# The last four units of the two-tile output products done tile by tile, in a two-block transformer kernel

## The chip, the cores and the metric

The kernel runs on one core of one Trainium2 chip. The metric is the time of one execution on the device, in microseconds, as the median of several runs.

## The reference

Everything is fp32 and the width is 1024. First a block of two layers on 256 positions: normed rows through an attention mixer and an output product, then a gated feed-forward product. Then a second block of two layers on the 256 positions and on 256 context positions; each of its sub-layers is computed like this, with `j` = 0 a feed-forward, 1 a mixer (attention and a gated spatial product), 2 a feed-forward:

```python
def adaln_in(s, g_pre, shift, scale):
    return rmsnorm(s, g_pre) * (1 + scale) + shift
def adaln_out(s, y, g_post, gate, weight):
    return s + weight * gate * rmsnorm(y, g_post)
def ffn_sublayer(s, mod, j, g_pre, g_post, wg, wu, wd):
    y = adaln_in(s, g_pre, mod[..., 3 * j, :, :], mod[..., 3 * j + 1, :, :])
    return adaln_out(s, swiglu(y, wg, wu, wd), g_post, mod[..., 3 * j + 2, :, :], FFN_RES)
```

So the output of a sub-layer needs the mean square of a whole row of `y` before it can be added to `x`, and the next sub-layer needs the mean square of the whole new row of `x` before its first product.

## The kernel before, in words

The program is one list of ten sub-layers (`SUBS`, numbered from 0). Positions lie in tiles of 128 rows: tiles 0 and 1 are the 256 positions, 2 and 3 the context. From sub-layer 4 on the tiles form two streams, the leading one (`LEAD`, tiles 2 and 3) and the trailing one (`TRAIL`, tiles 0 and 1). Sub-layers 4 to 7 carry two tiles per stream up to their end (`tt` is 4); they are followed by sub-layers 5 to 8, which begin with two tiles per stream. These are four handovers.

Every product is fp32 in three passes: each operand is split into a rounded high part and a low part, and the matmuls are high times high, high times low and low times high. Weights come in units of 128 x 1024 through a ring of four slots: a DMA fills `raw`, ScalarE makes `whi` (`split_hi`, L1003), VectorE makes `wlo` (`split_lo`, L1478). A slot is free again when the trailing stream has used the unit (`unit_done`).

A sub-layer has a wide part and a tall part. The wide part multiplies the transposed input (`xhi`, `xlo`) with chunks of four units, per chunk first the leading and then the trailing stream. The tall part is the output product. It adds up 8 or 22 units in PSUM, two banks per tile, banks 0 to 3 for the leading stream and 4 to 7 for the trailing one. Its units are taken in groups, in each group first a leading pass and then a trailing pass (`tall_pass`); a unit is 12 matmuls of 128 x 512 (two tiles, two halves, three products). Its activations are split per unit and stream into `ahi` and `alo` (`share_hi` L1015, `share_lo` L1701), in four places that the two streams use in turn, so that a share of the trailing pass waits for the leading pass's unit of the same number.

The order on each engine is written out by hand; semaphores join them. At a handover, for each stream:

- ScalarE squares the finished tile half by half with a running sum (`square_y`, L1104), VectorE multiplies it by the gain into `rows` (`add_y2`, L1624), GpSimd takes the inverse root (`inverse_root`, L2154), VectorE adds to `x` (L1633). ScalarE and VectorE never read the same PSUM half at once, and wait for one another between the halves.
- ScalarE squares the new row (`square_x`, L1089), GpSimd takes the root again, VectorE writes the normed row into `rows` (`normed_row`, L1519).
- TensorE transposes the normed rows into PSUM (`transposes_in`, L585, 8 per tile). Those of the leading stream stand ahead of the last unit of the trailing tall pass, those of the trailing stream ahead of unit 3 of the next sub-layer's first wide pass.
- ScalarE and VectorE turn the transposed pieces into the wide operand (`operand_hi`, `operand_lo`): eight pieces of 128 x 256, each scaled and shifted into `fbuf` (pieces 2, 3, 6, 7 on ScalarE, L1031; 0, 1, 4, 5 on VectorE, L1533), rounded (L1041) and the rest taken (L1543). The first wide unit waits for pieces 0 to 3 to be scaled and 0 and 1 to be split, unit `u` for pieces up to `2u + 1`. The next sub-layer's first four weight units are split in between.

## Time and profile before

| | |
|---|---|
| median of 3 runs | 2564.03 us (2563.63 to 2567.45) |
| the profiled execution | 2570.65 us, span 2568.8 us |
| TensorE busy | 2464.2 us (96%), 11536 matmuls |
| VectorE, ScalarE, GpSimd busy | 1145.1 (45%), 1064.4 (41%), 167.4 (7%) |
| mean granted TensorE clock | 0.980 |

The span is from the first to the last instruction that the profiler saw; the execution's own time has 1.85 us more around it. A matmul's end in the profile is modelled, and successive matmuls overlap, so work on TensorE is read from the starts. A granted clock of 1.00 is 2.4 GHz and 0.50 is 1.2 GHz.

### The profile page before, as it was taken

What the parts mean: (1) busy time and instruction counts of PE and PEld (TensorE: products, weight loads), DVE (VectorE), ACT (ScalarE), POOL (GpSimd) and SP (SyncE); (2) the same over time, 40 slices, a digit from 0 to 9 for tenths busy, and PEclk for the clock granted to TensorE, in tenths of its full rate; (3) what the DMA queues carried; (4) which work ended last, traced back from release to release, by engine and by line L of the source; (5) the groups of instructions that cost most, each with busy time, mean ns of one, the idle gap of its engine ahead of it and who ended that gap; (6) DMA issues with size and microseconds to landing.
All of it is one profiled execution on the core that took longest, in us unless ns stands there. A gap on an engine that the chain in (4) does not pass through costs nothing. (4 is left out here: it accounts for less than half of the span.)

```text
span 2568.8 us, 29909 instructions
## 1 busy us (share of the span) xinstructions
PE 2464.2 (96%) x11536; PEld 1939.5 (76%) x11536; DVE 1145.1 (45%) x1960; ACT 1064.4 (41%) x1945; POOL 167.4 (7%) x205
## 2 busy tenths in 40 slices
PE   8999999999999999999989999999999999987998
PEld 6766777766877778877677777887778887766777
DVE  5554455634552223354745222345222335455455
ACT  6443456434542223344545222334222334454544
POOL 1100003000010000022101000001000001310000
PEclk9999999999999999999989999999999999997999
DMA  5557654387534533232103444332432222312554
GB/s 207 184 205 286 229 180 141 123 302 281 189 125 163 173 122 99 91 114 66 58 25 131 157 171 163 100 107 74 174 109 95 99 87 94 115 58 74 172 181 147
DMA packets 118733, 364.40 MB, mean 142 GB/s; under 512 B 11072, under 2 KB 11712, under 8 KB 118592
## 3 DMA queue, kind: packets, MB, share of 16 engines
q1 hardware_dynamic: 116336, 355.62, 40.4%
q0 software_dynamic: 2256, 6.86, 1.1%
q8 instruction: 93, 1.52, 0.2%
q14 instruction: 48, 0.39, 0.1%
HBM read 361.35 MB, written 1.09 MB: 141 GB/s over the span
## 5 line engine op out<-in xcount | busy, mean ns | idle before, releaser
L1478 DVE TENSOR_TENSOR wlo<-raw,whi 128x1024 fp32r<-128x1024 f32 x524 | 644.0, 1234 | 620.1 <-ACT whi L1003 615.5
L562 PE MATMUL ps<-whi,xhi 128*128 128x512 f32 x2096 | 854.6, 408 | 12.5 <-DVE xlo L1570 5.0
L562 PE MATMUL ps<-whi,xlo 128*128 128x512 f32 x2096 | 823.6, 393 | 0.0
L562 PE MATMUL ps<-wlo,xhi 128*128 128x512 f32 x2096 | 821.8, 392 | 0.0
L1003 ACT CAST whi<-raw 128x1024 fp32r<-128x1024 f32 x524 | 549.2, 1051 | 511.0 <-PE ps L562 502.5
L562 PEld LDWEIGHTS ps<-whi,xhi 128*128 128x128 f32 x2096 | 397.9, 190 | 151.8 <-issue 66.1
L562 PEld LDWEIGHTS ps<-whi,xlo 128*128 128x128 f32 x2096 | 396.4, 189 | 87.9
L562 PEld LDWEIGHTS ps<-wlo,xhi 128*128 128x128 f32 x2096 | 398.2, 190 | 73.4
L562 PE MATMUL ps<-whi,ahi 128*128 128x512 f32 x952 | 375.8, 395 | 12.0 <-DVE alo L1701 7.7
L562 PE MATMUL ps<-whi,alo 128*128 128x512 f32 x952 | 373.1, 392 | 0.0
L562 PE MATMUL ps<-wlo,ahi 128*128 128x512 f32 x952 | 372.9, 392 | 0.0
L562 PEld LDWEIGHTS ps<-whi,ahi 128*128 128x128 f32 x952 | 180.1, 189 | 51.4 <-issue 5.9
L562 PEld LDWEIGHTS ps<-whi,alo 128*128 128x128 f32 x952 | 180.2, 189 | 38.1
L562 PEld LDWEIGHTS ps<-wlo,ahi 128*128 128x128 f32 x952 | 180.5, 190 | 36.5
L1692 DVE TENSOR_TENSOR hrow<-sgate,ps 128x256 f32<-128x256 f32 x154 | 58.6, 416 | 299.4 <-ACT sgate L1156 298.0
L1015 ACT CAST ahi<-hid 128x128 fp32r<-128x128 f32 (+1 forms) x264 | 86.7, 351 | 218.2 <-PE ps L562 218.0
L2154 POOL TENSOR_TENSOR rstd<-ms,mhalf 128x1 f32<-128x1 f32 (+1 forms) x55 | 41.3, 751 | 2000.4 <-DVE ms L1628 1430.1
L1701 DVE TENSOR_TENSOR alo<-hid,ahi 128x128 fp32r<-128x128 f32 (+1 forms) x264 | 88.6, 355 | 179.2 <-ACT ahi L1015 179.2
L1164 ACT COPY hid<-ps 128x256 f32<-128x256 f32 x198 | 67.0, 372 | 190.1 <-PE ps L621 190.1
L1156 ACT ACTIVATE sgate<-ps 128x256 f32<-128x256 f32 x154 | 51.5, 379 | 175.8 <-PE ps L562 175.8
L562 PE MATMUL ps<-mraw,cstat 128*32 128x512 f32 x576 | 76.7, 605 | 0.0
L621 PEld LDWEIGHTS ps<-ident,hrow 128*128 128x128 f32 x396 | 48.2, 140 | 33.3 <-DVE hrow L1689 14.2
(153 smaller groups left out, 1409.4 us busy)
## 6 DMA issues: line engine op xcount, KB each, us to landing
raw<-in_w SPq DMA_DIRECT2D x524, 512.0 KB, 3.8
mraw<-in_w_mod SPq DMA_DIRECT2D x72, 1024.0 KB, 6.6
grow<-gains POOLq DMA_DIRECT2D x11, 512.0 KB, 5.3
x<-in_x SPq DMA_DIRECT2D x2, 512.0 KB, 5.2
x<-in_ctx SPq DMA_DIRECT2D x1, 1024.0 KB, 7.8
out<-x SPq DMA_DIRECT2D x2, 512.0 KB, 2.6
rmask<-in_rmask SPq DMA_DIRECT2D x1, 768.0 KB, 4.9
ws<-in_ws POOLq DMA_DIRECT2D x2, 256.0 KB, 5.9
```

The source lines that it names most:

```text
L562: return nc.tensor.matmul(o, lhsT, rhs, start=start, stop=stop, skip_group_check=True)
L621: last = nc.tensor.transpose(bank(wide_bank(s, c, st, i), P * h, P * h + P), hrow[:, 2 * st + i, P * h:P * h + P], ident[:, :])
L1003: nc.scalar.copy(whi[:, slot, :], raw[:, slot, :]).then_inc(hi_done, 1)
L1015: nc.scalar.copy(ahi[:, w * aslot:w * aslot + w], src[:, row, P * tiles[0]:P * tiles[0] + w]).then_inc(a_hi_done, 1)
L1156: nc.scalar.activation(sgate[:, 2 * st + i, :], bank(wide_bank(s, c, st, i), 0, 256), ACT.Silu, **late).then_inc(silu_done, 1)
L1164: nc.scalar.copy(hid[:, 2 * c:2 * c + 2, P * t:P * t + P], src).then_inc(chunk_taken, 1)
L1478: nc.vector.tensor_tensor(wlo[:, slot, :], raw[:, slot, :], whi[:, slot, :].bitcast(F32), ALU.subtract).then_inc(w_split, 1)
L1692: nc.vector.tensor_tensor(hrow[:, 2 * st + i, :], sgate[:, 2 * st + i, :], up, ALU.mult).then_inc(gate_done, 1)
L1701: nc.vector.tensor_tensor(alo[:, w * aslot:w * aslot + w], src[:, row, P * tiles[0]:P * tiles[0] + w], ahi[:, w * aslot:w * aslot + w].bit ...
L2154: nc.gpsimd.tensor_tensor(rstd[:, m0:m], ms[:, m0:m], mhalf[:, m0:m], ALU.pow).then_inc(rstd_ready, 1)
```

## The change

In sub-layers 4 to 7 the last group of the tall part (four units, `by_tile`) is done in both passes first for the stream's first tile in all four units and then for its second tile. The first tile of each stream is therefore complete in the middle of the pass, and a unit counts as done when its second tile is. The leading transposes stand ahead of the last two units of the second tile, with the same twelve matmuls behind them as before. `square_y` and `add_y2` are cut into functions of one tile. On ScalarE and VectorE, output, addition and new row of each tile are put elsewhere: the leading first tile's among the trailing shares, the trailing first tile's ahead of and inside the next operand's pieces, the trailing second tile's wholly inside them. GpSimd takes the roots in the new order. Sub-layers 8 and 9 and the first block keep their order.

```diff
--- before.py
+++ after.py
+def by_tile(s, g):
+    return s["tt"] == 4 and g == len(s["groups"]) - 1
...
-                for k in group:
+                turns = [(k, (0, 1)[:len(tiles)]) for k in group]
+                if by_tile(s, g):
+                    turns = [(k, (i,)) for i in range(2) for k in group]
+                for k, which in turns:
...
+                    if by_tile(s, g):
+                        if nxt is not None and st == TRAIL and k == s["k"] - 2 and which == (1,):
+                            transposes_in(nxt, LEAD)
+                    elif nxt is not None and st == TRAIL and k == s["k"] - 4 + before_the_end(nxt):
                         transposes_in(nxt, LEAD)
...
-                    for i, t in enumerate(tiles):
+                    for i in which:
...
                         if final and i < len(tiles) - 1:
                             last.then_inc(y_ready, 1)
-                    last.then_inc(unit_done, 1)
+                    if len(tiles) - 1 in which:
+                        last.then_inc(unit_done, 1)
...
-            def operand_hi(s, st):
+            def operand_hi(s, st, trail=None):
...
                     scaled(2)
                     high(0)
                     high(1)
+                    if trail:
+                        square_x(trail["tall"][TRAIL][0], X_AT[trail["i"], trail["tall"][TRAIL][0]])
                     scaled(3)
                     high(2)
                     if st == LEAD:
                         split_hi(s["u_wide"] + 2)
-                    for k in (3, 4, 5):
+                    high(3)
+                    if trail:
+                        square_tile(trail, TRAIL, 1)
+                    for k in (4, 5):
                         high(k)
                     if st == LEAD:
                         split_hi(s["u_wide"] + 3)
                     scaled(7)
                     high(6)
                     high(7)
+                    if trail:
+                        square_x(trail["tall"][TRAIL][1], X_AT[trail["i"], trail["tall"][TRAIL][1]])
...
+            def square_tile(s, st, i):
+                tiles = s["tall"][st]
+                t = tiles[i]
+                if i < len(tiles) - 1:
+                    act.wait_ge(y_ready, n["y"] + 1)
+                    n["y"] += 1
+                else:
+                    act.wait_ge(unit_done, DONE[s["u_tall"] + s["k"] - 1, st])
+                for h in range(2):
...
+                    nc.scalar.activation(squares[:, t, CH * h:CH * h + CH], bank(tall_bank(st, i) + h), ACT.Square,
+                                         scale=D ** -0.5, accum_out=sqy[:, t, h:h + 1]).then_inc(sqy_halves, 1)
+                n["z"] += 1
             def square_y(s, st):
-                tiles = s["tall"][st]
...
+                for i in range(len(s["tall"][st])):
+                    square_tile(s, st, i)
...
+                if s is not None and s["tt"] == 4:
+                    if st == LEAD:
+                        square_tile(s, LEAD, 1)
+                        square_x(tiles[1], X_AT[s["i"], tiles[1]])
+                        square_tile(s, TRAIL, 0)
+                        split_hi(nxt["u_wide"])
+                        split_hi(nxt["u_wide"] + 1)
+                    operand_hi(nxt, st, s if st == LEAD else None)
+                    return
                 if s is not None and s["blk"] == 2:
                     square_y(s, st)
...
+                        if by_tile(s, g) and st == TRAIL:
+                            square_tile(s, LEAD, 0)
+                            for k in group[:3]:
+                                share_hi(s, k, TRAIL)
+                            square_x(s["tall"][LEAD][0], X_AT[s["i"], s["tall"][LEAD][0]])
+                            share_hi(s, group[3], TRAIL)
                             continue
...
-            def operand_lo(s, st):
+            def operand_lo(s, st, trail=None):
...
                     scaled(1)
                     low(0)
                     low(1)
+                    if trail:
+                        mean_square(trail["tall"][TRAIL][0])
+                        split_lo(s["u_wide"] + 1)
                     dve.wait_ge(xs_ready, s["xs0"][st] + 2)
                     scaled(4)
                     scaled(5)
@@ -1554,12 +1597,20 @@
                     if st == LEAD:
                         split_lo(s["u_wide"] + 2)
                     low(3)
+                    if trail:
+                        normed_tile(trail, TRAIL, 0)
+                        out_tile(trail, TRAIL, 1)
                     low(4)
                     low(5)
+                    if trail:
+                        add_tile(trail, TRAIL, 1)
                     if st == LEAD:
                         split_lo(s["u_wide"] + 3)
                     low(6)
                     low(7)
+                    if trail:
+                        mean_square(trail["tall"][TRAIL][1])
+                        normed_tile(trail, TRAIL, 1)
...
+            def out_tile(s, st, i):
+                dve.wait_ge(grow_ready, 16 * n["g"])
+                if i < len(tiles) - 1:
+                    dve.wait_ge(y_ready, n["y"] + 1)
+                    n["y"] += 1
+                else:
+                    dve.wait_ge(unit_done, DONE[s["u_tall"] + s["k"] - 1, st])
+                for h in (1, 0):
...
+                    nc.vector.tensor_tensor(rows[:, t, CH * h:CH * h + CH], bank(tall_bank(st, i) + h),
+                                            grow[:, ctx_of(tiles), CH * h:CH * h + CH], ALU.mult).then_inc(z_halves, 1)
+                n["z"] += 1
+                dve.wait_ge(sqy_halves, 2 * n["z"])
+                nc.vector.scalar_tensor_tensor(ms[:, t:t + 1], sqy[:, t, 0:1], EPS, sqy[:, t, 1:2], ALU.add,
+                                               ALU.add).then_inc(ms_ready, 1)
+            def add_tile(s, st, i):
+                t = s["tall"][st][i]
+                dve.wait_ge(z_halves, 2 * n["z"])
+                rstd_wait()
+                nc.vector.scalar_tensor_tensor(x[:, t, :], rows[:, t, :], rstd[:, t:t + 1], x[:, t, :],
+                                               ALU.mult, ALU.add).then_inc(x_ready, 1)
+
+            def normed_tile(s, st, i):
+                t = s["tall"][st][i]
+                dve.wait_ge(x_ready, X_AT[s["i"], t])
+                normed_row(t)
...
+                for i in range(len(s["tall"][st])):
+                    out_tile(s, st, i)
+                for i in range(len(s["tall"][st])):
+                    add_tile(s, st, i)
...
+                if s is not None and s["tt"] == 4:
+                    if st == LEAD:
+                        out_tile(s, LEAD, 1)
+                        normed_tile(s, LEAD, 0)
+                        add_tile(s, LEAD, 1)
+                        mean_square(tiles[1])
+                        normed_tile(s, LEAD, 1)
+                        out_tile(s, TRAIL, 0)
+                        split_lo(first)
+                        add_tile(s, TRAIL, 0)
+                    operand_lo(nxt, st, s if st == LEAD else None)
+                    return
...
+                        if by_tile(s, g) and st == TRAIL:
+                            out_tile(s, LEAD, 0)
+                            share_lo(s, group[0], TRAIL)
+                            share_lo(s, group[1], TRAIL)
+                            add_tile(s, LEAD, 0)
+                            share_lo(s, group[2], TRAIL)
+                            share_lo(s, group[3], TRAIL)
+                            mean_square(s["tall"][LEAD][0])
+                            continue
...
                 for st in (LEAD, TRAIL):
+                    if s["tt"] == 4:
+
+                        for t in s["tall"][st]:
+                            inverse_roots([t, t])
+                        continue
```

On VectorE, what stands between the last shares of the trailing pass and the next operand, at the first handover, before (`alo` are shares, `wlo` weight splits, `ms` a mean square, `rows<-ps,grow` the output by the gain, `rows<-x,rstd` the normed row):

```order
L1624 TENSOR_TENSOR rows<-ps,grow 128x512 x2
L1628 SCALAR_TENSOR_TENSOR ms<-sqy 128x1
L1624 TENSOR_TENSOR rows<-ps,grow 128x512 x2
L1628 SCALAR_TENSOR_TENSOR ms<-sqy 128x1
L1633 SCALAR_TENSOR_TENSOR x<-rows,rstd,x 128x1024 x2
L1507 TENSOR_SCALAR ms<-sq 128x1
L1519 TENSOR_SCALAR rows<-x,rstd 128x1024
L1507 TENSOR_SCALAR ms<-sq 128x1
L1519 TENSOR_SCALAR rows<-x,rstd 128x1024
L1478 TENSOR_TENSOR wlo<-raw,whi 128x1024 x2
```

and the beginning of the same stretch in the change, from the first instruction behind the leading shares:

```order
L1675 TENSOR_TENSOR rows<-ps,grow 128x512 x2
L1679 SCALAR_TENSOR_TENSOR ms<-sqy 128x1
L1779 TENSOR_TENSOR alo<-hid,ahi 128x256 x2
L1687 SCALAR_TENSOR_TENSOR x<-rows,rstd,x 128x1024
L1779 TENSOR_TENSOR alo<-hid,ahi 128x256 x2
L1547 TENSOR_SCALAR ms<-sq 128x1
L1675 TENSOR_TENSOR rows<-ps,grow 128x512 x2
L1679 SCALAR_TENSOR_TENSOR ms<-sqy 128x1
L1559 TENSOR_SCALAR rows<-x,rstd 128x1024
L1687 SCALAR_TENSOR_TENSOR x<-rows,rstd,x 128x1024
L1547 TENSOR_SCALAR ms<-sq 128x1
L1559 TENSOR_SCALAR rows<-x,rstd 128x1024
```

The leading first tile's output now stands ahead of the trailing shares and its addition between them; the second tile's output follows all of them, each tile's normed row and addition alternate, and no weight split stands here any more.

On ScalarE, the operand of the next sub-layer's leading stream, before (`fbuf` are scaled pieces, `xhi` the high parts, `whi` weight splits, `squares` the squares of a finished tile of `y`, `rows,sq<-x` the square of a new row):

```order
L1031 ACTIVATE fbuf<-ps,modT,acol 128x256
L1041 CAST xhi<-fbuf 128x256 x2
L1031 ACTIVATE fbuf<-ps,modT,acol 128x256
L1041 CAST xhi<-fbuf 128x256
L1003 CAST whi<-raw 128x1024
L1041 CAST xhi<-fbuf 128x256 x3
L1003 CAST whi<-raw 128x1024
L1031 ACTIVATE fbuf<-ps,modT,acol 128x256 x2
L1041 CAST xhi<-fbuf 128x256 x2
L1104 ACTIVATE squares,sqy<-ps 128x512 x4
```

and in the change, from the trailing first tile's squares on:

```order
L1123 ACTIVATE squares,sqy<-ps 128x512 x2
L1015 CAST whi<-raw 128x1024 x2
L1043 ACTIVATE fbuf<-ps,modT,acol 128x256
L1053 CAST xhi<-fbuf 128x256 x2
L1108 ACTIVATE rows,sq<-x 128x1024
L1043 ACTIVATE fbuf<-ps,modT,acol 128x256
L1053 CAST xhi<-fbuf 128x256
L1015 CAST whi<-raw 128x1024
L1053 CAST xhi<-fbuf 128x256
L1123 ACTIVATE squares,sqy<-ps 128x512 x2
L1053 CAST xhi<-fbuf 128x256 x2
L1015 CAST whi<-raw 128x1024
```

Two weight splits stand directly ahead of the operand and behind the trailing first tile's squares; the square of its new row is between the first high parts and the next scaled piece, and the second tile's squares are in the middle of the high parts.

On VectorE, the same operand before (`xlo` are the low parts):

```order
L1533 TENSOR_SCALAR fbuf<-ps,acol,modT 128x256 x2
L1543 TENSOR_TENSOR xlo<-fbuf,xhi 128x256 x2
L1533 TENSOR_SCALAR fbuf<-ps,acol,modT 128x256 x2
L1543 TENSOR_TENSOR xlo<-fbuf,xhi 128x256
L1478 TENSOR_TENSOR wlo<-raw,whi 128x1024
L1543 TENSOR_TENSOR xlo<-fbuf,xhi 128x256 x3
L1478 TENSOR_TENSOR wlo<-raw,whi 128x1024
L1543 TENSOR_TENSOR xlo<-fbuf,xhi 128x256 x2
```

and in the change:

```order
L1573 TENSOR_SCALAR fbuf<-ps,acol,modT 128x256 x2
L1583 TENSOR_TENSOR xlo<-fbuf,xhi 128x256 x2
L1547 TENSOR_SCALAR ms<-sq 128x1
L1518 TENSOR_TENSOR wlo<-raw,whi 128x1024
L1573 TENSOR_SCALAR fbuf<-ps,acol,modT 128x256 x2
L1583 TENSOR_TENSOR xlo<-fbuf,xhi 128x256
L1518 TENSOR_TENSOR wlo<-raw,whi 128x1024
L1583 TENSOR_TENSOR xlo<-fbuf,xhi 128x256
L1559 TENSOR_SCALAR rows<-x,rstd 128x1024
L1675 TENSOR_TENSOR rows<-ps,grow 128x512 x2
L1679 SCALAR_TENSOR_TENSOR ms<-sqy 128x1
L1583 TENSOR_TENSOR xlo<-fbuf,xhi 128x256 x2
```

A weight split, a normed row and the second tile's output came in between the low parts.

## Rows read from the trace of the kernel before

**Rows 1.** The page: busy time of each engine, its share, instructions.
```profile
PE 2464.2 (96%) x11536; PEld 1939.5 (76%) x11536; DVE 1145.1 (45%) x1960; ACT 1064.4 (41%) x1945; POOL 167.4 (7%) x205
```

**Rows 2.** Timeline of TensorE, first handover: start, duration, engine, line, instruction, idle before.
```profile
1111.78 0.39 PE L562 MATMUL ps<-whi,alo 128*128 128x512 f32 x1
...
1118.20 0.47 PE L562 MATMUL ps<-whi,xhi 128*128 128x512 f32 x1 [0.33 <-ACT fbuf L1031]
...
1126.15 0.39 PE L562 MATMUL ps<-wlo,xhi 128*128 128x512 f32 x1
1126.38 0.39 PE L562 MATMUL ps<-whi,xlo 128*128 128x512 f32 x1
...
1130.94 1.10 PE L585 MATMUL ps<-ident,rows 128*128 128x128 f32 x8 [4.17 <-DVE rows L1519]
...
1134.11 0.78 PE L562 MATMUL ps<-whi,xhi 128*128 128x512 f32 x1
1134.68 0.63 PE L562 MATMUL ps<-wlo,xhi 128*128 128x512 f32 x1
```

**Rows 3.** Timeline of TensorE at the second, third and fourth handover.
```profile
1366.56 0.39 PE L562 MATMUL ps<-whi,alo 128*128 128x512 f32 x1
...
1389.06 0.78 PE L562 MATMUL ps<-whi,xhi 128*128 128x512 f32 x1
...
1770.49 0.39 PE L562 MATMUL ps<-whi,alo 128*128 128x512 f32 x1
...
1792.82 0.78 PE L562 MATMUL ps<-whi,xhi 128*128 128x512 f32 x1
...
2163.11 0.39 PE L562 MATMUL ps<-whi,alo 128*128 128x512 f32 x1
...
2185.97 0.78 PE L562 MATMUL ps<-whi,xhi 128*128 128x512 f32 x1
```

**Rows 4.** Table by stretch: length, busy time (count) per engine, TensorE clock, DMA.
```profile
1131.90:1135.30 3.40, 2.95 (x13) 2.62 (x12) 2.21 (x5) 1.57 (x5) 1.91 (x2) 0.50 0.29 2
...
1384.50:1391.30 6.80, 5.57 (x21) 5.13 (x22) 4.27 (x10) 3.41 (x9) 3.10 (x4) 0.50 0.17 2
```

**Rows 5.** Timelines of ScalarE, VectorE and GpSimd, leading stream of the first handover.
```profile
1104.36 0.60 ACT L1104 ACTIVATE squares<-ps 128x512 f32<-128x512 f32 x1
...
1104.85 0.19 ACT L1104 ACTIVATION_READ_ACCUMULATOR squares<-ps 128x1 f32 x1
...
1106.34 1.28 DVE L1624 TENSOR_TENSOR rows<-ps,grow 128x512 f32<-128x512 f32 x2
...
1106.51 0.56 POOL L2154 TENSOR_TENSOR rstd<-ms,mhalf 128x1 f32<-128x1 f32 x1 [366.80 <-DVE ms L1628]
...
1107.65 1.04 ACT L1003 CAST whi<-raw 128x1024 fp32r<-128x1024 f32 x1
...
1107.87 1.28 DVE L1633 SCALAR_TENSOR_TENSOR x<-rows,rstd,x 128x1024 f32<-128x1024 f32 x1
...
1108.02 1.55 POOL L2154 TENSOR_TENSOR rstd<-ms,mhalf 128x1 f32<-128x1 f32 x1 [0.95 <-DVE ms L1628]
...
1109.19 1.06 ACT L1089 ACTIVATE rows<-x 128x1024 f32<-128x1024 f32 x1 [0.51 <-DVE x L1633]
...
1111.68 0.75 DVE L1519 TENSOR_SCALAR rows<-x,rstd 128x1024 f32<-128x1024 f32 x1 [0.73 <-POOL rstd L2154]
...
1113.89 2.35 DVE L1478 TENSOR_TENSOR wlo<-raw,whi 128x1024 fp32r<-128x1024 f32 x2
...
1114.81 0.57 ACT L1031 ACTIVATE fbuf<-ps,modT,acol 128x256 f32<-128x256 f32 x1 [1.80 <-PE ps L585]
...
1116.16 0.99 DVE L1533 TENSOR_SCALAR fbuf<-ps,acol,modT 128x256 f32<-128x256 f32 x2
...
1116.73 0.86 ACT L1041 CAST xhi<-fbuf 128x256 fp32r<-128x256 f32 x2 [1.36 <-DVE fbuf L1533]
...
1117.17 0.88 DVE L1543 TENSOR_TENSOR xlo<-fbuf,xhi 128x256 fp32r<-128x256 f32 x2
```

42 lines of the change are left out of this document (7 added, 35 removed).

## The prediction

> **What bounds the kernel now.** I read the page first: TensorE is busy for 96% of the span and no other engine for half of it [rows 1]. So the time is TensorE's queue, and a change that adds or removes no matmul can only move the places where that queue stands still. Four of them are touched: the handovers out of the four sub-layers whose products have two tiles per stream (4 to 5, 5 to 6, 6 to 7, 7 to 8 in the program's count). I read TensorE's timeline at the first. One 512-column matmul follows another every 0.227 us (1126.15 to 1126.38 in [rows 2]), so a half unit of 6 takes 1.36 us, a unit of 12 takes 2.72, a group of four 10.88; 8 transposes take 0.87 (1.10 shown, less the tail that overlaps). The reader is to see in [rows 2]: 6.42 us from the last matmul before the leading stream's transposes (1111.78) to the first wide matmul (1118.20), in which lie 4.69 of work (0.23, 16 transposes, 12 matmuls), so 1.73 lost, 0.33 of it idle at its very end; and an idle time of 4.17 before the trailing stream's transposes, ended by VectorE's normed row. I add up the whole: from 1111.78 to the first matmul of wide unit 3 (1134.11) there are 0.23 + 1.74 (16 transposes) + 2.72 + 8.16 + 1.74 = 14.60 us of work, and 22.33 passed: 7.73 lost. The same difference at the others is 22.50, 22.33 and 22.86 [rows 3], so 7.9, 7.7 and 8.3 are lost; together 31.6. After that come matmuls at the half clock: in [rows 4] the granted clock is 0.50, that is 1.2 GHz, for 3.4 us at the first handover and for 6.8 at the second; the third is like the first, the fourth like the second. From unit 3 on this costs about 0.6, 1.2, 0.6 and 1.9 us (0.35 for the first matmul, 1134.11 to 1134.68 in [rows 2], and 0.2 for each further one until the low stretch ends, whose duration is 0.63 there against 0.39). All that the change can reach is 31.6 + 4.3 = 36 us, 1.4% of the time.
>
> **Why VectorE and ScalarE are late.** Each tile's new row is a chain through both, one tile after another. Prices from the first handover [rows 5]: square of half a tile 0.68 with its accumulator read (next may start after 0.58), gain product of half a tile 0.68 (0.60), the two squares' sum 0.16, root on GpSimd 0.56, addition 1.28, square of x 1.15 (1.06), normed row 0.75, weight split 1.04 on ScalarE (0.95) and 1.22 on VectorE (1.14), scaled piece 0.57 on ScalarE and 0.54 on VectorE, high part 0.41 (0.31), low part 0.42 (0.34), and a share, of the same size, the same on both. A handoff between engines costs 0.03 to 0.1. One root took 1.55 instead of 0.56: VectorE's addition had begun 0.15 before it and ended at 1109.15, and the root ended 0.41 later. I charge that delay wherever a root meets a long VectorE instruction on SBUF.
>
> **The change, on one handover.** I set T = 0 at the start of the leading pass of the last group, 1092.96 in the trace (1111.78 + 0.23 less seven units of 2.72), and lay each engine's new list out in order with the prices above. As a test, the same bookkeeping on the old lists gives TensorE waits of 0.56, 0.68, 0.59, 0.13, 4.55 and 0.68, 7.2 us, and the trailing transposes at T = 38.18; the trace has them at 1130.94, T = 37.98. It is 0.2 us late after 38 and does not know the clock.
>
> *The leading pass.* TensorE's matmuls are the same ones in another order, so its work costs nothing more. It asks for share and weights of the last unit at T = 4.08 instead of 8.16. Their split ends at 2.81 (slot free at 0.20, share 0.31, split 1.04, then 1.22): 1.1 us of cover, no wait. The same 12 matmuls stand behind the leading transposes.
>
> *Leading stream.* Tile 0 is finished at 5.44 and not 8.16. Its squares and gain products run 5.64 to 7.05, its addition stands behind two shares whose slots come free only with units 0 and 1 of tile 1, and runs 9.15 to 10.43; square 10.47 to 11.62. The last trailing share is queued behind that square: 11.53 to 12.40 over both engines, wanted at 14.96, so covered. Tile 1: products 12.39 to 13.67, addition 15.18 to 16.46 (its root meets the normed row of tile 0), square to 17.65, normed row 18.57 to 19.33. TensorE wants tile 0's row at 19.04 (there since 14.66) and tile 1's at 19.91. Both waits go: 1.1 us gained.
>
> *Trailing tile 0.* Finished at 16.32, but VectorE takes it up after that normed row: products 19.24 to 20.53. ScalarE stands in its second square until 20.65, then makes the first two weight splits to 22.54. VectorE: split 21.63 to 22.85, addition 22.76 to 24.05, two scaled pieces to 24.96, and ScalarE's two high parts to 25.40. Now ScalarE's square of x (25.31 to 26.46) stands ahead of the scaled piece 3, which ends at 26.92. The first wide matmul needs that piece: it starts at 27.06, where TensorE was ready at 23.51. **A wait of 3.56 us in place of 0.59**: this is what the change pays.
>
> *Inside the first three wide units.* VectorE: split of unit 1 to 27.78, pieces 4 and 5 to 28.70, low part 2, split of unit 2 to 30.17, low part 3 to 30.51, so unit 1 starts at 30.65 instead of 29.78 (0.86 lost). Normed row of trailing tile 0, 30.42 to 31.17; products of tile 1, 31.09 to 32.37, with ScalarE held in its second square to 32.50; high parts 4 and 5, low parts to 33.59, so unit 2 starts 0.36 late at 33.73. Addition 33.50 to 34.79, split of unit 3 to 35.92, square of x 35.50 to 36.65, root, normed row 37.57 to 38.33.
>
> *Trailing transposes.* Unit 2 ends at 36.45, tile 0's row is long there, 8 transposes to 37.32, tile 1's start at 38.38: 1.06 lost. Unit 3 starts at 39.25, on the trace's clock 1132.21 and not 1134.11. So 5.8 us are lost to waits where 7.7 were.
>
> **The sum.** Four times 5.84 is 23.4 against 31.6: 8.2 us. The low clock goes from unit 3, for by then TensorE has worked nearly without a pause since T = 27: up to 4.3 us. It may fall behind the 3.56 wait instead. There a low stretch of 3.4 us costs 1.7 us of matmul time, but the waits of 0.86, 0.36 and 1.06 behind it are ends of the VectorE and ScalarE chain, which does not wait for TensorE there, and swallow 2.3; I charge 0.3 per handover for the cases of 6.8 us. The bookkeeping's bias gives 0.2 each back. 8.2 + 4.3 - 1.2 + 0.8 = 12.1, rounded to **12 us**. The profiled execution (2570.65, span 2568.8) would become 2558.6; it stands 6.6 above the median of 2564.03, so I predict **2552 us**. Weight loads into the ring start 0.7 to 6 us later (they follow the VectorE splits), and are first wanted 13 us after the handover; I cost them at nothing. No engine gets an instruction more.
>
> **The root and the shared port.** The row of 1.55 us shows the delay [rows 5]. The Trainium skill, "SBUF — State Buffer", section "SBUF: two separate sides", says that GpSimd and a VectorE instruction with two SBUF inputs take one port pair by an exclusive lock, so that the later one blocks fully; by that rule the change is worse than the old order, since its roots meet a VectorE that works without gaps. The trace agrees for the one root that met an addition.
>
> **Rivals.**
> *The roots wait for VectorE to stand still* (a mechanism of the new order: additions and splits back to back). Trailing tile 0's root is issued at T = 26.73 inside 4 us of unbroken VectorE work; if it only gets through when VectorE stops for it, its normed row is 0.6 late, and the root of tile 1 makes its addition 0.6 late. For: the 1.55 row. Against: between two instructions there was room in every other row. 1.2 us on four handovers takes 5 of the 12: **2557**. Chance 0.20, two fifths of it inside 0.2%.
> *The low clock is not swallowed*: it falls at the 3.56 wait for 6.8 us everywhere, 3.4 lost less 2.3, and the transposes run in it too (1.7 more): 2.8 more on each handover, which takes 11: **2563**, no change. Chance 0.08.
> *The clock stays low through the whole handover*, the way to slower: four waits within 12 us instead of one, each feeding the next low stretch. From the wait at T = 23.5 on, low for 13.6 us costs 6.8 less 2.3 swallowed, 4.5 on top of 5.8: 10.3 against 9.0, 4 times 1.3 slower: **2569**. It decides from some 11 us of low clock per handover. Against it: no stretch in [rows 4] is over 6.8, and the clock stayed full behind the 1.73 us lost around the leading transposes [rows 2]. The Trainium skill, "TensorE: Matmul & The Clock Gate", section "HAM oscillation — how this bites in real kernels", has this as a rule: pauses between short batches bring every batch back to the cold clock; no run here shows it for waits as short as 1 us. Chance 0.08.
> *The first wait is shorter* because handoffs overlap more than I charge, or a root is not delayed by a normed row (0.5 less): each us on the chain is 4 us of time, so 17 or more are saved: **2546**. Chance 0.09.
> The forecast keeps 0.55.
>
> **Numbers.** A measurement of this kernel tells about 0.2% (5.1 us) from no change. Faster by more: 0.55 + 0.12 + 0.09 = 0.76; within it 0.16; slower 0.08. For 8 in 10 the range must hold the forecast, the rival of the roots and part of the shorter wait: from 2546 (18 saved) to 2560.5 (3.5 saved).
>
> **What would show it.** In the changed profile, at each handover: no idle time, or under 0.2 us, before the leading transposes; about 3.3 to 3.6 us ended by ScalarE's scaled piece or VectorE before the first wide matmul; no 4 us wait before the trailing transposes but about 1 us, before the second tile's; low clock, if any, directly behind the first wide matmul and not at unit 3. From the end of the leading transposes' last unit to wide unit 3, 15.7 us. I am wrong if the long wait is gone without a new one ahead of the first wide unit (more gain), or if the chain to the trailing tile 1's row takes longer than T = 39.5.

## The result, and the profile after

The change made the kernel faster by about as much as forecast. It takes 2549.33 us (median of four executions, 2546.97 to 2551.56) where the kernel before takes 2565.62 (2563.63 to 2567.45): a ratio of 0.9937, 95% interval 0.9919 to 0.9954, 16.3 us less; 2552 was forecast. The four executions of the changed kernel are two pairs, at 2547.0 and 2551.5, and the median lies between them. Profiled executions: 2570.65 us before, 2547.14 after (span 2545.3, mean granted clock 0.988 where it was 0.980).

TensorE is still the only full engine. The page of the changed kernel, against [rows 1]:

```profile
PE 2447.3 (96%) x11536; PEld 1926.0 (76%) x11536; DVE 1145.1 (45%) x1960; ACT 1062.0 (42%) x1945; POOL 165.1 (6%) x205
```

TensorE's timeline at the first handover of the changed kernel, against [rows 2]; the columns are the same:

```profile
1106.93 0.39 PE L567 MATMUL ps<-whi,alo 128*128 128x512 f32 x1
...
1107.17 1.91 PE L590 MATMUL ps<-ident,rows 128*128 128x128 f32 x16
...
1115.09 0.47 PE L567 MATMUL ps<-whi,xhi 128*128 128x512 f32 x1 [3.27 <-ACT fbuf L1043]
...
1118.67 0.47 PE L567 MATMUL ps<-whi,xhi 128*128 128x512 f32 x1 [0.57 <-DVE xlo L1583]
...
1121.74 0.47 PE L567 MATMUL ps<-whi,xhi 128*128 128x512 f32 x1
...
1124.56 1.03 PE L590 MATMUL ps<-ident,rows 128*128 128x128 f32 x8
1126.35 1.09 PE L590 MATMUL ps<-ident,rows 128*128 128x128 f32 x8 [0.76 <-DVE rows L1559]
1127.20 0.48 PE L567 MATMUL ps<-whi,xhi 128*128 128x512 f32 x1
```

The 16 leading transposes follow the last matmul at once. The wait of 4.17 us ahead of the trailing transposes is gone; in its place stand idle times of 3.27 us ahead of the first wide matmul, 0.57 ahead of unit 1, next to nothing ahead of unit 2, and 0.76 ahead of the second tile's transposes. From 1106.93 to unit 3 at 1127.20 pass 20.27 us, against 22.33 before.

The same two matmuls at the second, third and fourth handover, against [rows 3]:

```profile
1359.63 0.40 PE L567 MATMUL ps<-whi,alo 128*128 128x512 f32 x1
...
1379.90 0.48 PE L567 MATMUL ps<-whi,xhi 128*128 128x512 f32 x1
...
1760.31 0.40 PE L567 MATMUL ps<-whi,alo 128*128 128x512 f32 x1
...
1780.57 0.47 PE L567 MATMUL ps<-whi,xhi 128*128 128x512 f32 x1
...
2150.33 0.39 PE L567 MATMUL ps<-whi,alo 128*128 128x512 f32 x1
...
2170.59 0.48 PE L567 MATMUL ps<-whi,xhi 128*128 128x512 f32 x1
```

They are 20.27, 20.26 and 20.26 us apart. Less the 14.60 us of work, 5.7 us are lost at each handover, where 7.73, 7.9, 7.7 and 8.3 were.

The granted clock, in the table by stretch of the changed kernel, against [rows 4]: the whole neighbourhood of the first and second handover, and the only low stretches at the third and fourth.

```profile
1085.00:1145.00 60.00, 55.33 (x258) 45.16 (x257) 38.42 (x65) 32.83 (x68) 11.74 (x17) 1.00 0.34 111
1345.00:1400.00 55.00, 50.29 (x240) 41.03 (x239) 36.05 (x64) 31.11 (x68) 9.06 (x12) 1.00 0.42 142
1769.00:1772.40 3.40, 3.40 (x9) 2.65 (x8) 3.40 (x7) 1.45 (x4) 0.58 (x1) 0.50 0.46 154
2158.10:2161.50 3.40, 3.02 (x7) 2.50 (x8) 3.40 (x6) 2.37 (x6) 1.45 (x1) 0.50 0.37 110
```

At the first two the clock is full (2.4 GHz) throughout; at the others it is at 1.2 GHz for 3.4 us behind the first wait, and still the four handovers take the same time to 0.01 us. The later waits show why: those ahead of units 1 and 2 (0.73 and 0.23 us from start to start at the first handover) are gone at the third and fourth, and the one ahead of the second tile's transposes shrank from 0.76 to 0.52.

```profile
2169.74 1.09 PE L590 MATMUL ps<-ident,rows 128*128 128x128 f32 x8 [0.52 <-DVE rows L1559]
```

VectorE, ScalarE and GpSimd of the changed kernel, the chain that ends the first wait, against [rows 5]:

```profile
1102.13 1.00 POOL L2242 TENSOR_TENSOR rstd<-ms,mhalf 128x1 f32<-128x1 f32 x1 [0.96 <-DVE ms L1679]
...
1107.30 1.28 DVE L1675 TENSOR_TENSOR rows<-ps,grow 128x512 f32<-128x512 f32 x2
...
1108.02 0.60 ACT L1123 ACTIVATE squares<-ps 128x512 f32<-128x512 f32 x1 [1.73 <-DVE rows L1675]
1108.61 1.99 ACT L1015 CAST whi<-raw 128x1024 fp32r<-128x1024 f32 x2
1109.67 1.23 DVE L1518 TENSOR_TENSOR wlo<-raw,whi 128x1024 fp32r<-128x1024 f32 x1 [0.78 <-ACT whi L1015]
1110.82 1.28 DVE L1687 SCALAR_TENSOR_TENSOR x<-rows,rstd,x 128x1024 f32<-128x1024 f32 x1
1112.01 0.99 DVE L1573 TENSOR_SCALAR fbuf<-ps,acol,modT 128x256 f32<-128x256 f32 x2
...
1113.35 1.05 ACT L1108 ACTIVATE rows<-x 128x1024 f32<-128x1024 f32 x1
1114.40 0.55 ACT L1043 ACTIVATE fbuf<-ps,modT,acol 128x256 f32<-128x256 f32 x1
...
1114.76 1.46 POOL L2242 TENSOR_TENSOR rstd<-ms,mhalf 128x1 f32<-128x1 f32 x1 [5.24 <-DVE ms L1547]
```

The forecast's T = 0 is 1088.12 here (1106.93 + 0.23 less seven units). It had trailing tile 0's products at 19.24, the addition at 22.76, the square of x at 25.31 and the first wide matmul at 27.06; the rows give 19.18, 22.70, 25.23 and 26.97.

### The profile page after: what moved, and what is told of

Same layout as the page of the kernel before. It is cut to its first block and busy times, and to the rows that moved or that the text cites. A ratio compares the mean times of both kernels' runs of the same rounds, so it can differ in the third digit from the quotient of the medians.

```text
span 2545.3 us, 29957 instructions
## 1 busy us (share of the span) xinstructions
PE 2447.3 (96%) x11536; PEld 1926.0 (76%) x11536; DVE 1145.1 (45%) x1960; ACT 1062.0 (42%) x1945; POOL 165.1 (6%) x205
```

## Where the rest of the time went

For all kernels below I use one measure: at each handover, the time from the start of the 84th instruction ahead of the leading transposes to that of the 25th behind the trailing ones, less 156 matmuls of 0.2267 us and 32 transposes of 0.109. This difference counts waits and low clock together. Where I give a wait "from start to start", it is the spacing of two starts less that of two successive instructions; the idle time in a row is shorter, since it begins at the modelled end of the instruction before. Summed over the four handovers it is 36.17 us before (8.40, 9.04, 8.43, 10.30) and 23.13 after (5.78, 5.78, 5.79, 5.77): **13.0 us**, where 12 were forecast. The profiled executions differ by 23.5 and the medians by 16.3, so 3 to 10 us are elsewhere. By the spacings above, 9.0 of the 13.0 lie ahead of unit 3; the other 4 lie behind it, where the kernel before had its low clock. TensorE runs the same 11536 instructions in both, so I took the stretches between the same numbers of them. The two traces of each kernel, profiled time first (the second ones are experiments below):

```
                                     before  before    after   after
profiled time                       2570.65 2567.11  2547.14 2551.46
four handovers, lost                  36.17   36.12    23.13   23.85
instructions     0 to  2216          493.01  489.86   489.10  488.47
              2216 to  4909          584.66  584.70   583.54  583.38
              5153 to  6132          200.05  200.05   200.59  199.00
             10336 to 10630           64.17   62.58    57.09   63.82
```

Instructions 10336 to 10630 are the mixer of sub-layer 8, which the change doesn't touch. There the changed kernel's first trace has a low stretch of 3.4 us, and the kernel before one of 20.5:

```profile
2308.30:2311.70 3.40, 3.00 (x7) 2.45 (x8) 1.67 (x8) 0.00 (x0) 0.00 (x0) 0.50 0.00 0
```

```profile
2316.30:2336.80 20.50, 18.05 (x74) 16.98 (x75) 8.00 (x34) 3.72 (x13) 1.64 (x1) 0.50 0.00 0
```

These instructions alone take 7.1 us less in the changed kernel's profiled execution. The experiments on the repeated traces ask whether the change earned it.

## Experiments

**TensorE's order alone.** The kernel before with tile-by-tile turns and the leading transposes at their new place; VectorE, ScalarE and GpSimd keep their old order.

```
+                turns = [(k, (0, 1)[:len(tiles)]) for k in group]
+                if by_tile(s, g):
+                    turns = [(k, (i,)) for i in range(2) for k in group]
```

> TensorE's tile-by-tile order of the last group alone, with the old orders on ScalarE, VectorE and GpSimd. Theory (the handover ends with a chain through ScalarE and VectorE, and TensorE's order by itself brings nothing): the trailing shares now wait for the second tile's units and everything behind them stays put, so the leading chain starts late: waits of about 2.7, 0.7, 0.6, 0.1, 4.6, 0.7 us, 9.3 us per handover where the kernel before has 7.2 by the same bookkeeping, and the half clock at unit 3 stays. Four handovers: about 8 us slower than before, 2573 to 2575. Rival (the gain comes from finishing the first tile in the middle of the pass): faster than before by 4 us or more.

Measured: 2570.18 us, ratio 1.0019 (1.0010 to 1.0029): 5.5 above the 2564.69 of the kernel before in that session, slower as expected but short of the 8 that I expected. Handovers 45.45 us, 9.3 more; in its profiled execution the last mixer gave 7 back (57.12 us for 64.17). TensorE's timeline of this kernel:

```profile
1110.67 3.51 PE L590 MATMUL ps<-ident,rows 128*128 128x128 f32 x16 [2.50 <-DVE rows L1531]
...
1129.11 3.67 PE L590 MATMUL ps<-ident,rows 128*128 128x128 f32 x16 [3.83 <-DVE rows L1531]
```

The first wait came as forecast (2.66 in start-to-start times). The trailing one is shorter, about 4.0 where 4.6 was expected, and those of 0.6 and 0.7 are down to 0 and 0.1. Low clock ahead of a wait that VectorE ends would do that, but no run separates it from the bookkeeping's error (4.55 for 4.33 in the kernel before). And 10.2 us of low clock per handover, three times the 3.4 of the first handover before, slow the transposes themselves (3.51 us for 16 against 1.91). TensorE's order brings nothing without the others.

**Leading stream alone.** The changed kernel with the trailing stream's early work put back behind the leading stream's.

```
-                        square_tile(s, TRAIL, 0)
...
-                        out_tile(s, TRAIL, 0)
                         split_lo(first)
-                        add_tile(s, TRAIL, 0)
+                        split_lo(first + 1)
```

> The leading stream's part of the change alone (TensorE's order of both passes, output, addition and rows of both leading tiles in the new places); the trailing tiles' work stands in one piece behind the operand, as in the kernel before. Theory: the waits ahead of the leading transposes and of the first wide unit go (0 to 0.2 us left), the wait of 4.4 us before the trailing transposes stays whole, 0.7 before the second tile's. By waits alone that is 5.4 us per handover, less than the 5.8 of the full change; but the one long wait is again followed by the half clock, which here nothing swallows: 1.4 to 3.5 us on each handover. So about 7 to 8 us lost per handover, 4 to 8 us faster than before and 4 to 9 slower than the full change: 2554 to 2561. Rival (the trailing part buys time by itself, the clock has little to do with it): the waits at full clock are longer than 5.8 us per handover. Rival (the trailing part is worthless): as fast as the full change within 1 us per handover.

Measured: 2554.28 us, ratio 0.9956 (0.9942 to 0.9971). Handovers 28.17 us (7.40, 7.52, 6.09, 7.16), 8.0 less than before. No wait ahead of the leading transposes, none over 0.1 us ahead of the wide units, and the old one at its old place:

```profile
1106.62 1.91 PE L590 MATMUL ps<-ident,rows 128*128 128x128 f32 x16
...
1123.92 3.67 PE L590 MATMUL ps<-ident,rows 128*128 128x128 f32 x16 [4.26 <-DVE rows L1562]
```

So 8 of the 13 us come from the leading stream's part and 5 from the trailing one, but not by shorter waits. By waits alone this kernel is the better one: from start to start it has 4.42 and 0.10 us at the first handover, where the full change has 3.43, 0.73, 0.23 and 0.92. What it loses beyond them is low clock, 6.8 us of it at three handovers and 3.4 at the third, which also loses the least (6.09). The trailing part moves the long wait forward, to where the low clock behind it is taken up by the waits that follow.

**Output in the gap.** The trailing tile's first product goes ahead of the leading tile 1's mean square and its second ahead of the normed row, where VectorE waits for ScalarE and the root.

```
-                        mean_square(tiles[1])
-                        normed_tile(s, LEAD, 1)
-                        out_tile(s, TRAIL, 0)
+                        out_tile(s, TRAIL, 0, "first")
+                        mean_square(tiles[1])
+                        out_tile(s, TRAIL, 0, "second")
+                        normed_tile(s, LEAD, 1)
+                        out_tile(s, TRAIL, 0, "sum")
```

> The full change, and the gain products of trailing tile 0 moved ahead of the normed row of leading tile 1 (the first before its mean square, the second before the row), where VectorE stands waiting for ScalarE and GpSimd. Theory (one chain through both engines from trailing tile 0 to the last normed row sets the end, each us on it is a us of each handover): all of it 1.2 us earlier, the wait ahead of the first wide unit 2.3 us where the full change has 3.4, the later ones the same 0.7, 0.3, 0.9: 1.2 us per handover, 5 us less than the full change. Rival (the waits within the wide units are set by the weight splits and not by the chain): less than 0.4 us per handover.

Measured: 2547.13 us (2544.58 to 2548.42), ratio 0.9927 (0.9912 to 0.9942). Handovers 15.90 us, 1.8 less each and not 1.2; the wait is 1.61 from start to start, where 2.3 was expected:

```profile
1109.82 0.47 PE L567 MATMUL ps<-whi,xhi 128*128 128x512 f32 x1 [1.45 <-ACT fbuf L1043]
```

My bookkeeping charges a root that meets a long VectorE instruction on SBUF. The root of trailing tile 0's output began 0.02 us ahead of the weight split here, and neither is longer than usual by more than 0.03, so that delay did not come:

```profile
1104.36 0.54 POOL L2257 TENSOR_TENSOR rstd<-ms,mhalf 128x1 f32<-128x1 f32 x1 [1.30 <-DVE ms L1667]
```

```profile
1104.38 1.25 DVE L1518 TENSOR_TENSOR wlo<-raw,whi 128x1024 fp32r<-128x1024 f32 x1
```

But of 7.2 us saved at the handovers the profiled time kept 1.2. Instructions 10336 to 10630 took 63.95 us here, with 20.5 us of low clock. Either this order disturbs the last mixer, or that stretch comes and goes by itself; this is taken up below.

**Square of x behind the scaled piece.** ScalarE does the piece that the first wide matmul waits for first.

```
-                    if trail:
-                        square_x(trail["tall"][TRAIL][0], X_AT[trail["i"], trail["tall"][TRAIL][0]])
                     scaled(3)
+                    if trail:
+                        square_x(trail["tall"][TRAIL][0], X_AT[trail["i"], trail["tall"][TRAIL][0]])
```

> The full change, with ScalarE's square of trailing tile 0's new row behind the scaled piece 3 and not ahead of it. It is the instruction that stands ahead of the piece for which the first wide unit waits. Theory (the end is set by the chain, what happens to TensorE in between is swallowed): the first wait falls from 3.4 to about 2.4 us, the second grows from 0.7 to about 2.3, and as the chain gets 0.5 us longer the handover loses 0.5 more in sum: 2 us slower than the full change on four handovers. Rival (the wait ahead of the first wide unit is a cost by itself): 1 us per handover faster, 4 us in sum.

Measured: 2557.46 us, ratio 0.9972 (0.9960 to 0.9983). At the first and third handover the two waits are as forecast, 2.4 and 2.2 from start to start:

```profile
1112.67 0.47 PE L567 MATMUL ps<-whi,xhi 128*128 128x512 f32 x1 [2.23 <-ACT fbuf L1043]
...
1117.74 0.47 PE L567 MATMUL ps<-whi,xhi 128*128 128x512 f32 x1 [2.07 <-DVE xlo L1583]
```

At the second and fourth, 3.4 us of low clock lie between the two, and the second wait is 0.7: again the clock is paid out of it. Handovers 25.58, 2.4 us more than in the changed kernel, close to the forecast of 2. The wait that goes returns one unit later, behind the same square. The other 6 us of the median's difference lie outside the handovers; in the profiled execution 7.0 of them are in the last mixer (64.05 us for 57.09).

**Extra work in the chain, and ahead of it.** Two more products of half a tile, in the trailing stream's tile-0 output or in the leading stream's.

```
+                        for _ in range(2 if s["tt"] == 4 and (st, i) == (TRAIL, 0) else 0):
+                            link(nc.vector.tensor_tensor(rows[:, t, 0:CH], bank(tall_bank(st, i)),
+                                                         grow[:, ctx_of(tiles), 0:CH], ALU.mult))
```

> The changed kernel with two extra gain products of half a tile (about 0.68 us each, nothing reads them twice) on VectorE inside the trailing stream's tile-0 output at each handover. My theory (VectorE's chain through this output to the first weight split ends TensorE's first wait, with 0.66 us of slack in front of the second half, where it waits for ScalarE's squares): the wait ahead of wide unit 0 grows from 3.4 to about 4.1 us, the others stay, 6.5 us per handover, 3 us in all. Rival A (VectorE has no slack there): 4.8 us, 7.2 per handover, 5.5 us in all. Rival B (the first wait is set by ScalarE's squares and parts): it stays at 3.4 us.

> The changed kernel with two extra gain products of half a tile (about 0.68 us each) on VectorE inside the LEADING stream's tile-0 output, which lies some 12 us ahead of TensorE's first wait. Theory (VectorE stands idle behind this output, waiting for ScalarE's squares and TensorE's units, and takes the extra work in there): the waits stay at 3.4, 0.7, 0.2 and 0.9 us, 5.8 per handover. Rival (VectorE's work is one unbroken chain from there to the first weight split): the first wait is 1.36 us longer, 7.2 per handover.

Measured, one execution each: 2558.79 and 2555.71 us. In the trailing output the first wait is 4.37 where it was 3.43, 0.94 longer, between the 0.70 of my theory and the 1.36 of the rival; the handovers are 6.71, 6.93, 7.41 and 6.71 us. The trace shows that the theory came near for a wrong reason:

```profile
1109.43 1.46 POOL L2245 TENSOR_TENSOR rstd<-ms,mhalf 128x1 f32<-128x1 f32 x1 [3.65 <-DVE ms L1682]
```

```profile
1111.00 1.28 DVE L1690 SCALAR_TENSOR_TENSOR x<-rows,rstd,x 128x1024 f32<-128x1024 f32 x1 [0.52 <-POOL rstd L2245]
```

VectorE had more slack than I thought, and its weight split began only 0.34 us later. But the root now met that split, took 1.46 us where it had taken 0.54, and VectorE stood idle for 0.52 ahead of the addition. So by the trace a delayed root did reach TensorE here, for some 0.6 us at the first handover.

In the leading output, where I expected nothing, the first wait is 3.73, 0.30 longer, and the handovers are 6.10, 6.77, 6.09 and 6.77. The trace of that kernel shows the path: the leading addition comes 0.30 us later behind the output, ScalarE's square of x with it, and behind that square stand the last share and the squares of tile 1. VectorE's gaps take 1.06 of the 1.36 us, not all. The chain that ends the first wait thus begins some 20 us ahead of that end, on both engines.

**The same kernel once more.** No edit.

> The changed kernel once more, with no edit, for a second trace. Two of its four executions took 4.4 us more than the two others. Theory (half-clock stretches outside the handovers come and go between executions of one kernel): the handovers again lose 5.8 us each, 23.1 in all, whatever the time; if the profiled execution takes about 2551.5 us, the difference lies in the last mixer (stretch of 57.09 us in the first trace) and ahead of the first handover. Rival (the handovers themselves vary, by a wait of another length): a slower execution has handovers of 6.5 us and more.

> The kernel before once more, with no edit. The profiled execution of before took 2570.65 us where the median is 2564 to 2566. Theory: its handovers lose again 8.4 to 10.3 us each, about 36 in all, and any difference in time lies in the half-clock stretches outside them: 584.66 us ahead of the first handover and 64.17 us in the last mixer can come out at 583.6 and 57 to 59. Rival: the handovers take less, 30 us in all.

Measured: the changed kernel 2548.26 us (2546.66 to 2551.46), ratio 0.9932 (0.9916 to 0.9949). Its profiled execution took 2551.46 us, 4.3 more than the first trace, and the handovers 23.85 (5.79, 6.48, 5.79, 5.79). The three others had 3.4 us of low clock each and lost nothing by it; the second had 6.8, and the waits behind it couldn't swallow it all: 0.7 passed through. To that extent the rival of the expectation is right too. The difference is in the last mixer, 63.82 us for 57.09, less 2.4 us gained ahead of the second handover. Its low stretch:

```profile
2296.50:2317.00 20.50, 17.27 (x73) 16.37 (x74) 8.66 (x36) 4.50 (x14) 1.71 (x2) 0.50 0.01 6
```

The kernel before took 2567.11, with handovers of 36.12 against 36.17. Its last mixer stayed long, 62.58 us, and instructions 2216 to 4909 took what they had; of the 3.5 us between its two traces, 3.15 are in the first 2216 instructions. I had expected them elsewhere.

**Early output at three handovers, or at the fourth only.**

```
-                        out_tile(s, TRAIL, 0, "first")
+                        if s["i"] != 7:
+                            out_tile(s, TRAIL, 0, "first")
...
+                        else:
+                            mean_square(tiles[1])
+                            normed_tile(s, LEAD, 1)
+                            out_tile(s, TRAIL, 0)
```

> The early output's order at the first three handovers and the changed kernel's at the fourth. It asks what decides the half-clock stretch of about 20 us in the last mixer (2291 to 2316 us in the early output's trace, absent in the changed kernel's), which cost 7 us there. Both theories: 3.97, 3.97, 3.97 and 5.78 us at the handovers, 5.4 us less than in the changed kernel. Theory (where the stretch falls in time against the low clock before it decides, so that a small shift of all that follows can bring it or take it away, and one kernel can show both): the last mixer's stretch can come out at 57 or at 64 us here and in the kernel with early output in the fourth handover, and the two need not differ; 2542 or 2549 us. Rival (the order of the fourth handover itself decides): 57 us here, 2543 us, and 64 us in the other.

> The changed kernel's order at the first three handovers and the early output's at the fourth. Handovers 5.78, 5.78, 5.78 and 3.97 us, 1.8 us less than in the changed kernel. Theory (a shift in time decides): 57 or 64 us for the last mixer's stretch, whatever the other kernel shows; 2546 or 2553 us. Rival (the order of the fourth handover decides): 64 us here, 2553 us, while the kernel with the changed order in the fourth has 57.

Measured: 2547.86 us (2544.70, 2545.80, 2549.91, 2550.55) and 2548.88 (2546.08, 2546.17, 2551.60, 2552.19). The kernel before was at 2560.39 in that session, so the ratios are 0.9946 (0.9931 to 0.9961) and 0.9951 (0.9935 to 0.9967): no gain over the changed kernel can be told in the time. Handovers as forecast, 3.96, 3.95, 3.97, 5.77 and 5.79, 5.76, 5.77, 3.97. The last mixer has the long low stretch in both profiled executions:

```profile
2295.60:2316.10 20.50, 17.44 (x73) 16.54 (x74) 8.60 (x36) 4.34 (x14) 1.64 (x1) 0.50 0.01 6
```

```profile
2300.80:2317.90 17.10, 14.86 (x61) 13.78 (x61) 6.26 (x28) 3.01 (x11) 1.60 (x1) 0.50 0.00 1
```

The rival, that the fourth handover's order decides, asked for 57 us in the first of them; it was 63.88, and 62.57 in the other. The four times of each kernel are two pairs, 4 to 6 us apart. The two traces of the changed kernel show that the stretch comes and goes between executions of one kernel. What chooses it is not shown. Over all traces of this document the last mixer takes 57 to 58.5 us in four (the changed kernel's first, TensorE's order alone, the leading stream alone and the order below) and 62.5 to 64.2 in the nine others, and the loss at the handovers does not sort them: 45.5 us goes with the short one, 15.9 with the long one. Chance between executions is not all of it either, for the late square's six executions all took 2555.8 us or more, 4 above what the changed kernel's median and its handovers give.

**Another order on both engines.** The changed kernel with VectorE's and ScalarE's instructions at the handover in a list searched with the bookkeeping of the prediction. Behind the leading tile 1's addition:

```
+                        dve_turn = "xnL0 xL1 zT01 mqL1 zT00 mT0 xnL1 wn0 xT0 f0 f1 wn1 lo0 lo1 zT11 wn2 f4 mqT0 ..."
```

Here z is half an output product, m the squares' sum, x an addition, mq a mean square, xn a normed row, wn a weight split, f a scaled piece, lo a low part; L and T the stream.

> The changed kernel with the same instructions in another order on VectorE and ScalarE at the four handovers: the trailing stream's tile 0 is squared first on ScalarE (ahead of the weight splits), its two half tiles of output go between the leading tile 1's addition, mean square and new rows, and the leading halves, trailing additions and gain products are spread among the wide product's low and high parts. My theory (TensorE only waits there for the chain of VectorE work, so an order in which nothing it needs stands behind long work that it does not need removes most of the 5.8 us per handover): about 1.1 to 1.5 us are left at each, 17 to 18 us less in all than in the changed kernel, so 2532 us, from 2529 to 2537. Rival A (the time is given back outside the handovers, because half-clock stretches there fall differently, as 7 us of the early output's gain were): 2537 to 2541. Rival B (splitting the outputs into more, shorter turns makes the engines wait on one another where the changed kernel has them in blocks): waits of 3 us or more stay per handover, 2543 to 2550.

Measured: **2531.86 us** (2528.20 to 2532.57), 0.9881 (0.9864 to 0.9897) of the kernel before, which was at 2560.39 then. Handovers 1.27, 1.28, 1.28 and 1.26: 18.0 us less than in the changed kernel. TensorE's and VectorE's timelines of this kernel:

```profile
1107.87 1.91 PE L590 MATMUL ps<-ident,rows 128*128 128x128 f32 x16
...
1113.03 0.47 PE L567 MATMUL ps<-whi,xhi 128*128 128x512 f32 x1 [0.52 <-issue]
...
1121.56 2.07 PE L590 MATMUL ps<-ident,rows 128*128 128x128 f32 x16
```

```profile
1106.23 0.69 DVE L1714 TENSOR_TENSOR rows<-ps,grow 128x512 f32<-128x512 f32 x1
...
1107.80 1.23 DVE L1534 TENSOR_TENSOR wlo<-raw,whi 128x1024 fp32r<-128x1024 f32 x1
1108.95 1.28 DVE L1742 SCALAR_TENSOR_TENSOR x<-rows,rstd,x 128x1024 f32<-128x1024 f32 x1
...
1113.45 1.21 DVE L1534 TENSOR_TENSOR wlo<-raw,whi 128x1024 fp32r<-128x1024 f32 x1
```

The trailing products lie ahead of the leading normed row (VectorE's gaps filled), and the first weight split begins 0.07 us ahead of the leading transposes; in the changed kernel it began 2.50 behind them (1109.67). The waits left are 0.68, 0.11 and 0.10 us from start to start. The rivals, 2537 us or more, are refuted. This version beats both kernels.

## Why the prediction was right

*The measure and the bound.* TensorE's queue was the time: the losses at the handovers, 36.2 by trace and 36 by my count, are what the change could reach, and 13.0 of them went.

*The waits.* Forecast 3.56, 0.86, 0.36 and 1.06; measured at the first handover, start to start, 3.43, 0.73, 0.23 and 0.92. Each is 0.13 less, but that is not time gained: behind each wait the second matmul follows the first by 0.31 us and not 0.227. By the whole spacing a handover loses 5.67 us where 5.84 was forecast. Both waits of the leading transposes went, as said. The late square bears out what stands in the chain to 0.1 us a wait; in TensorE's order alone and the leading stream alone up to 0.7 us of a later wait is missing where the clock was low, and the extra work came within 0.3 of its forecast for another reason than mine. The term was 8.2 us, with 0.8 on top for the bookkeeping's bias; by the spacing against [rows 3] it is 9.0.

*The low clock.* The 4.3 us behind unit 3 went (4.1 by the difference of 13.0 and 9.0). I charged 0.3 per handover for low stretches behind the first wait, 1.2 in all; the first trace has no low stretches of over 3.4 us, and its two handovers with 3.4 us lost 5.79 and 5.77 where the two at full clock lost 5.78. The 6.8 us stretch of the second trace lost 0.7. So this term was 1.2 and measured 0 and 0.7, which is about the 1 us between the 12.1 of the sum and the 13.0 at the handovers, and the rival in which low clock is not swallowed is refuted. The Trainium skill, "TensorE: Matmul & The Clock Gate", section "HAM oscillation — how this bites in real kernels", has each short batch of matmuls behind a wait of about 3 to 5 us start at the cold clock. Of the waits in the changed kernel only the first is that long. Behind its 3.27 us of idle time the clock was full at the first two handovers of the changed kernel and at 1.2 GHz for 3.4 us at the two others, so this trace agrees for half of them; TensorE's order alone, with idle times of 2.50 and 3.83 us and 10.2 us low at each handover, agrees.

*The roots.* One met a normed row and took 1.00 us where 0.54 is usual, as charged. The root of trailing tile 0's new row met a weight split and took 1.46 (1114.76 above), but ended 0.40 after that split while VectorE went on with the next piece: it did not wait for VectorE to stand still, and its normed row, wanted later, was not held up. The waits of that rival are not there: it falls, and so does the slower one, which wanted over 11 us of low clock per handover (3.4 and 6.8 were seen). By the median alone the rival of the shorter first wait, 17 us saved, would fit 16.3 better than the forecast; its first wait is not there, 0.13 us shorter being far from the 1 us and more that it needs at each handover. The charge for met roots hangs on some 0.1 us of order: the early output escaped it (1.61 us of wait for 2.3 expected), the extra work in the trailing output ran into it.

*The step that was mis-sized* is the sum's last: that the difference of the profiled executions is the handovers alone, 12.1 us. It was 23.5, of which 13.0 at the handovers and 10.5 outside, 7.1 of that in the last mixer, which in the changed kernel falls either way from one execution to the next. Of the medians' 16.3 some 3 are outside. So the mechanism at the handovers is shown. That the median came within 2.7 us of the forecast is in part luck: it depends on how many executions fall into each of the two groups, at 2547.0 and 2551.5; both lie in the range. That the changed kernel draws the short mixer more often than the kernel before is possible (before's two traces have 62.6 and 64.2), but four traces don't show it; this stays open.

## To carry to other kernels

Where one engine is full and waits for a chain through two others, add up its lost time start to start, lay the chain out instruction by instruction, and move what the chain doesn't need out of it: the price of a wait is what stands in line ahead of the instruction that ends it, and moving one instruction can bring the wait back one unit later, as the late square did. Low clock directly ahead of waits that another engine's chain sets cost nothing here until it exceeded them (3.4 us free, 0.7 lost of 6.8), so a long wait is worth placing ahead of the short ones. Before crediting a change with all of a difference of some 5 us, take a second trace and split it into the part that the change touches and the rest.

## What I had not expected of the hardware

- Stretches of 13.7 to 20.5 us at 1.2 GHz in parts where TensorE is busy for 84% to 88% of them. The one in the last mixer was 20.5 us long in one execution of the changed kernel and 3.4 in another, and these instructions took 6.7 us more with it.
- A GpSimd instruction of 128x1 behind VectorE's normed row, which reads one tensor of SBUF, took 1.00 us and ended 0.40 after it; behind a weight split of two inputs it took 1.46, and where an addition waited for it (the extra work) that came to some 0.6 us of TensorE's wait. Where VectorE began a low part 0.05 us after it, or a weight split 0.02 after it, neither was longer than usual by more than 0.03 (0.54; 0.76 for two low parts; 1.25 for the split). In the reordered kernel a normed row that began 0.29 us after it did go with a longer one, 1.07 us, so the start alone does not decide.
